# Value product turned round: values as weights, two heads on two column halves, attention output born transposed

## The reference

```
first_block:
    proj = rms_norm(x, attn_norm_gain) @ w_in        # fq fk fv fg dq dk dv
    fox_o = forgetting_attention(fq, fk, fv, fg + bias)   # 16 heads of 64
    dil_o = dilated_attention(rope(dq), rope(dk), dv)     # 16 heads of 64, 3 patterns
    mixed = concat[rms_norm(fox_o, fox_out_gain), rms_norm(dil_o, dil_out_gain)]
    h = x + mixed @ w_out ;  h = h + peer(rms_norm(h, g)) ;  return rms_norm(h)
    # attention of one head:  p = softmax(q k^T / 8 + mask terms);  o = p @ v
second_block (its end):
    gate = sigmoid(rmsnorm(x, ple_norm_g) @ w_ple_gate)
    x = x + gate * (p @ w_ple_proj) ;  return rmsnorm(x, final_norm_g)
```

## Time and profile before

| | |
|---|---|
| median of 3 runs | 2812.62 us (2812.09 to 2813.28) |
| the profiled execution: its time | 2811.79 us |
| its span, first to last instruction | 2810.0 us |
| TensorE busy | 2790.0 us, 99% of the span |
| VectorE, ScalarE, GpSimd busy | 65%, 50%, 25% |
| TensorE's granted clock | 0.999 of full |
| attention's side work | about 174 to 355 us of the span |
| embedding gate | about 2697 to 2810 us |

### The profile page before, as it was taken

One profiled execution on the slowest core, in us unless ns is written; L12 is line 12 of the kernel. 1 busy time (PEld: TensorE's weight loads), 2 busy tenths in 40 slices (PEclk: granted clock), 3 DMA queues, 4 the chain that ended last, 5 costly groups with the idle time before them and its releaser, 6 DMA issues.

```text
span 2810.0 us, 39121 instructions
## 1 busy us (share of the span) xinstructions
PE 2790.0 (99%) x14986; PEld 2403.7 (86%) x14986; DVE 1824.3 (65%) x2904; ACT 1409.5 (50%) x1993; POOL 697.8 (25%) x365
## 2 busy tenths in 40 slices
PE   9999999999999999999999999999999999999998
PEld 7888888888888888888888888888888888999886
DVE  6566766877777755555555555566777876555554
ACT  5445654555555544454444444546655555444454
POOL 0000000488888888800000000001201111000000
PEclk9999999999999999999999999999999999999999
DMA  7653479877777777777677777765665546666664
GB/s 273 211 158 121 142 239 338 240 189 190 191 189 188 190 191 189 190 217 223 209 223 222 212 237 223 238 209 185 185 183 157 160 153 190 188 190 189 184 197 154
DMA packets 199018, 559.02 MB, mean 199 GB/s; under 512 B 53344, under 2 KB 69872, under 8 KB 195888
## 3 DMA queue, kind: packets, MB, share of 16 engines
q1 hardware_dynamic: 161744, 556.04, 63.6%
q0 software_dynamic: 36944, 0.41, 2.7%
q10 hardware_dynamic: 144, 0.07, 0.0%
HBM read 535.32 MB, written 21.12 MB: 198 GB/s over the span
## 4 chain that ended last, share of the span: by engine, by line
PE 93%; DVE 3%; ACT 2%; issue 1%; DMA 1%; POOL 0%; DVEq 0%; SPq 0%; ACTq 0%
PE bank L535 92%; DVE wlo L946 1%; ACT whi L1675 1%; PE bank L547 1%; DMA raw<-in_w_pq 0%; DMA raw<-in_w_dv 0%; DVE tmpc L949 0%; ACT EB L1675 0%; ACT L1675 0%; DVE aX L981 0%; DVE QKb L949 0%; DVE AT L1200 0%; ACT scr L1675 0%; DVE EB L1008 0%; DVE X L949 0%
## 5 line engine op out<-in xcount | busy, mean ns | idle before, releaser
L946 DVE TENSOR_TENSOR wlo<-raw,whi 128x1024 fp32r<-128x1024 f32 (+1 forms) x965 | 1188.9, 1234 | 852.7 <-ACT whi L1675 849.5
L1675 ACT ACTIVATE whi<-raw 128x1024 fp32r<-128x1024 f32 (+1 forms) x967 | 1017.3, 1054 | 992.7 <-PE bank L535 974.9
L535 PE MATMUL bank<-aX,whi 128*128 128x512 f32 (+1 forms) x4000 | 968.9, 392 | 0.8 <-DVE aX L981 0.8
L535 PE MATMUL bank<-whi,aX 128*128 128x512 f32 x3008 | 932.5, 390 | 0.5 <-DVE aX L949 0.4
L535 PEld LDWEIGHTS bank<-aX,whi 128*128 128x128 f32 (+1 forms) x4000 | 728.1, 188 | 142.0 <-issue 3.0
L535 PEld LDWEIGHTS bank<-whi,aX 128*128 128x128 f32 x3008 | 565.0, 188 | 119.3 <-DVE aX L949 1.5
L1635 POOL DMA_INDIRECT gate_scratch<-gate,place x256 | 585.7, 2288 | 256.1 <-DMA gate_scratch<-HB 178.4
L535 PE MATMUL bank<-wlo,aX 128*128 128x512 f32 x1504 | 585.5, 390 | 2.2 <-DVE wlo L946 2.2
L535 PEld LDWEIGHTS bank<-aX,wlo 128*128 128x128 f32 (+1 forms) x3984 | 513.3, 191 | 21.0 <-DVE wlo L946 0.8
L535 PE MATMUL bank<-aX,wlo 128*128 128x256 f32 (+1 forms) x3984 | 529.4, 284 | 0.3 <-DVE wlo L946 0.2
L535 PEld LDWEIGHTS bank<-wlo,aX 128*128 128x128 f32 x1504 | 282.6, 188 | 62.2 <-DVE wlo L946 4.2
(11 more groups left out here) (229 smaller groups left out, 1833.4 us busy)
## 6 DMA issues: line engine op xcount, KB each, us to landing
raw<-in_w_down SPq DMA_DIRECT2D x256, 512.0 KB, 3.7
raw<-in_w_up SPq DMA_DIRECT2D x256, 512.0 KB, 4.3
raw<-in_w_in SPq DMA_DIRECT2D x176, 512.0 KB, 3.8
raw<-in_w_out SPq DMA_DIRECT2D x32, 512.0 KB, 3.8
gate_scratch<-HB SPq DMA_DIRECT2D x16, 1024.0 KB, 7.6
raw<-in_w_pq SPq DMA_DIRECT2D x32, 512.0 KB, 5.4
raw<-in_w_o SPq DMA_DIRECT2D x32, 512.0 KB, 4.3
raw<-in_w_pg SPq DMA_DIRECT2D x32, 512.0 KB, 4.2
```

What stands on the lines that cost most here:

```text
L535: return e.matmul(o, lhsT, rhs, start=start, stop=stop, skip_group_check=True)
L946: e.tensor_tensor(wlo[:, s, 0:n], raw[:, r, 0:n], whi[:, s, 0:n].bitcast(F32), ALU.subtract).then_inc(s_lo, 1)
L1675: return e.activation(o, i, f, **k)
```

## The change

**Value product.** `VV` (128 keys x 64 features of head x) is now the weight and `PB` streams: 256 columns (both query blocks) for key block 0 and 128 for key block 1. Head 0 writes PSUM partitions 0 to 63, head 1 partitions 64 to 127 of the same bank, with the heads innermost in the loop. The output is features x tokens, so no transposes of `TM` follow: `MIX_TURN`, its TensorE transposes, `high_two` and `low_two` for dil and fox are gone, and so is `VR`. ScalarE writes the high part and VectorE the low part straight from the value product's bank (phase D), in `mD` and `mF`, which lie over dead parts of the query/key tiles and of `TM`.

**Normalization.** The reciprocal sum belongs to a token, which is now a column, so it is applied before the transposes: GpSimd multiplies `EB` by the reciprocals in two instructions per pair (2x128 and 2x256 columns), and phase C waits for it (`s_gn`). For f pairs the reciprocal moves to a phase B at +1, C to +3 and D to +4.

**Sums of squares.** ScalarE squares the value product's bank into `sq`, GpSimd adds the squares up in `acc` (14 additions of 128x256), and TensorE sums over the partitions by a product with ones (`mix_sums`, ticks 89 and 106). The eight 128x512 squares are gone.

**Embedding gate.** Group i's multiply, add and square are done inside group i+1's `pg` units, each behind a split (`gated`, `gated_square`); only the last group's stay at the end.

```diff
-MIX_TURN = {86: ("dil", 0), 87: ("dil", 1), 90: ("dil", 2), ...
-MIX_SQUARE = {84: ("dil", 0), 85: ("dil", 1), 102: ("fox", 0), 103: ("fox", 1)}
-MIX_SUM = {92: "dil", 104: "fox"}
+MIX_ROW = {89: "dil", 106: "fox"}
...
-        for phase, n in zip("ABCD", (0, 1, 3, 4)) if kind == "d" else zip("ACD", (0, 2, 3)):
+        for phase, n in zip("ABCD", (0, 1, 3, 4)):
...
             if phase == "C":
-                if kind == "d":
-                    w.wait_ge(s_cn, 4 * sum(k == "d" for k, _, _ in PAIRS[:q + 1]))
-                else:
-                    w.wait_ge(s_ex, 4 * q + 4)
+                w.wait_ge(s_gn, q + 1)
...
-                for t in range(2):
+                for kt in range(2):
                     for x in range(2):
-                        for kt in range(t + 1):
-                            ov = mm(b[:, 128 * t + 64 * x:128 * t + 64 * x + 64],
-                                    PB[:, 2 * (q % 3) + x, (t + kt) * 128:(t + kt) * 128 + 128],
-                                    VV[:, kt, vb + 64 * x:vb + 64 * x + 64], kt == 0, kt == t)
+                        ov = mm(b[64 * x:64 * x + 64, 128 * kt:256], VV[:, kt, vb + 64 * x:vb + 64 * x + 64],
+                                PB[:, 2 * (q % 3) + x, 256 * kt:256 + 128 * kt], kt == 0, kt == 1)
...
+        def mix_sums(name):
+            q = PLACE[name[0], 7]
+            w.wait_ge(s_sa, ADDED[q])
+            b = vacant(mfill[name])
+            for t in range(2):
+                sm = mm(b[:, t * 128:t * 128 + 128], acc[name[0]][:, t * 128:t * 128 + 128], ones[:, 0:128], True, True)
+            sm.then_inc(s_sm, 1)
...
             if phase == "D":                                  # VectorE
-                w.wait_ge(s_turn, 4 if q < 4 else 8)
-                tt(TM[...], banks[b][:, 0:256]..., d2[:, :, 4:6]..., ALU.mult).then_inc(s_free[b], 1)
+                w.wait_ge(s_ph, q + 1)
+                e.scalar_tensor_tensor(o[:, 256:512], banks[b][:, 0:256], cols[:, c:c + 1], o[:, 0:256].bitcast(F32),
+                                       ALU.mult, ALU.subtract).then_inc(s_free[b], 1)
...
+        def normalize(q):                                     # GpSimd
+            w.wait_ge(s_rd, q + 1)
+            for c, k in ((slice(0, 128), 4), (slice(128, 384), 5)):
+                p = E[:, :, c]
+                last = e.tensor_tensor(p, p, d2[:, :, k:k + 1].to_broadcast([128, 2, c.stop - c.start]), ALU.mult)
+            last.then_inc(s_gn, 1)
+        def add_squares(q, kind, pair):
+            if pair:
+                w.wait_ge(s_sqp, DONE.index(q) + 1)
+                w.wait_ge(s_sa, ADDED[q] - 1)
+                e.tensor_tensor(acc[kind], acc[kind], sq[:, ADDED[q] % 2, :], ALU.add).then_inc(s_sa, 1)
...
+            if phase == "D":                                  # ScalarE
+                w.wait_ge(s_ov, q + 1)
+                act(junk, banks[b][:, 0:256], ACT.Square).then_inc(s_sqp, 1)
+                w.wait_ge(s_turn, 8 if kind == "f" else 4)
+                if kind == "d":
+                    w.wait_ge(s_lg, 2 * over(q) + 2)
+                act(o[:, 0:256], banks[b][:, 0:256], ACT.Copy, scale=cols[:, c:c + 1]).then_inc(s_ph, 1)
...
         for i in range(4):                                    # VectorE, embedding gate
-            steps(G["pg", i])
-            ...  multiply and add of group i behind pp, for both token blocks
+            for j, u in enumerate(G["pg", i].units):
+                step(u)
+                if i and j < 2:
+                    gated(i - 1, j)
+            steps(G["pp", i])
+        for t in range(2):
+            gated(3, t)
```

More of the change, by code:

```diff
@@ L218, in _build @@
     rsin = attc[:, 912:928].rearrange("p (t i) -> p t i", t=2)
-    fz, fu, fw, fm = (fgs[:, i, :] for i in range(4))
+    fz, fu, fw, fm = (fgs[0:16, i, :] for i in range(4))
+    acc = {"d": fgs[:, 0, :], "f": fgs[:, 1, :]}
+    sq = fgs[:, 2:4, :]
     A.close()
     B_ = ExitStack()
-    alloc(B_, "below_VV", [128, 2 * 4096])
-    VR = alloc(B_, "VR", [128, 2, D], F32R)
-    alloc(B_, "below_dil", [128, 2 * 2048])
+    alloc(B_, "below_fox", [128, 4096])
+    mF = alloc(B_, "mF", [128, 8, 512], F32R)
+    alloc(B_, "below_dil", [128, 2 * 4096])
     mD = alloc(B_, "mD", [128, 8, 512], F32R)
@@ L319, in _build @@
                 hfill[q, phase] = [plan.side()]
-        if t in MIX_TURN:
-            plan.turn(*MIX_TURN[t], plan.side())
+        if t in MIX_ROW:
+            mfill[MIX_ROW[t]] = plan.side()
+    mfill["fox"] = plan.side()
     for name, part in (("wd", range(4, 8)), ("wf", range(4))):
@@ L404, in tile, with over @@
         if name == "dil":
-            return mD[:, kt, :]
+            return mD[:, kt // 2 + kt % 2 * 4, :]
         if name == "fox":
-            return VR[:, kt // 2, 1024 + kt % 2 * 512:1536 + kt % 2 * 512] if kt < 4 else aX[:, 8 + kt, :]
+            return mF[:, kt, :]
         return aX[:, mix_row(kt) if name == "mix" else kt, :]
[L410 to L413, removed]
+    PLACE = {(kind, pair): q for q, (kind, pair, _) in enumerate(PAIRS)}
+    DONE = [q for t in HEAD_TICKS for q, _, _, phase in HEADS[t] if phase == "D"]
+    ADDED = {q: n + 1 for n, q in enumerate(x for x in DONE if PAIRS[x][1])}
+    def over(q):
+        pair = PAIRS[q][1]
+        return max(PLACE["d", p] for p in (pair // 2 * 2, pair // 2 * 2 + 1))
     def decay_cols(p):
@@ L666, in tick @@
                         heads(q, kind, pair, phase)
-            if u in MIX_TURN:
-                mix_turn(*MIX_TURN[u])
+            if u in MIX_ROW:
+                mix_sums(MIX_ROW[u])
             if u == ROWS0 + 4:
@@ L974, in row_scale, with mix_scale @@
             e.reciprocal(st[:, o:o + 2], st[:, 20:22]).then_inc(s_rinv, 1)
+        def mix_scale(name, o):
+            j = next(sums)
+            b, _ = mfill[name]
+            w.wait_ge(s_sm, 1 if name == "dil" else 2)
+            e.tensor_copy(st[:, 16:18], banks[b][:, 0:256].rearrange("p (t c) -> p t c", t=2)[:, :, 0]).then_inc(s_free[b], 1)
+            evacuated(mfill[name])
+            e.tensor_scalar(st[:, 16:18], st[:, 16:18], 1.0 / 1024, EPS, ALU.mult, ALU.add).then_inc(s_rsum, 2)
+            w.wait_ge(s_root, j + 1)
+            e.reciprocal(st[:, o:o + 2], st[:, 20:22]).then_inc(s_rinv, 1)
         def low_two(name, kp):
@@ L1009, in heads @@
                                                ALU.add, ALU.min, d[:, t:t + 1]).then_inc(s_free[b] if t else s_mx, 1)
-            if phase == "B":
+            if phase == "B" and kind == "d":
                 for x in range(2):
@@ L1018, in heads @@
                 e.reciprocal(d2[:, :, 4:6], d2[:, :, 2:4]).then_inc(s_rd, 1)
-            if phase == "C" and kind == "f":
+            if phase == "B" and kind == "f":
                 w.wait_ge(s_ex, 4 * q + 4)
@@ L1240, in step @@
                     heads(q, kind, pair, phase)
[L1241 to L1246, removed]
+            if u in MIX_ROW:
+                mix_scale(MIX_ROW[u], 24 if MIX_ROW[u] == "dil" else 26)
             if u == G["dq", 0].first + 1:
@@ L1594, in _, with gated @@
                 tt(o, banks[b], o, ALU.add).then_inc(s_free[b], 1)
-        row_scale(4, D, 40, 8)
-        for i in range(4):
-            steps(G["pg", i])
[L1598 to L1611, removed]
+        row_scale(4, D, 36, 4)
+        def gated(i, t):
+            g = G["pp", i]
+            b, _ = g.fills[t]
+            o, x = scr2[:, t, i * 512:i * 512 + 512], X2[:, t, i * 512:i * 512 + 512]
+            if i == 3 and t == 0:
+                w.wait_ge(s_pt, 1)
+            else:
+                ready(g)
+            evacuated(G["pg", i].fills[t])
+            tt(o, banks[b], o, ALU.mult).then_inc(s_free[b], 1)
+            evacuated(g.fills[t])
+            tt(x, x, o, ALU.add).then_inc(s_x4, 1)
+        for i in range(4):
+            for j, u in enumerate(G["pg", i].units):
[5 more added lines that the diff above has]
+            gated(3, t)
+        row_scale(4, D, 44, 4)
         w.wait_ge(s_row2, 16)
@@ L1624, in _ @@
         w = Gate(e)
+        def normalize(q):
+            E, d2 = EB[:, 2 * (q % 3):2 * (q % 3) + 2, :], dn[:, 2 * (q % 3):2 * (q % 3) + 2, :]
+            w.wait_ge(s_rd, q + 1)
[8 more added lines that the diff above has]
+                e.tensor_tensor(acc[kind], acc[kind], sq[:, ADDED[q] % 2, :], ALU.add).then_inc(s_sa, 1)
+        for t in HEAD_TICKS:
+            for q, kind, pair, phase in HEADS[t]:
+                if phase == "B":
+                    normalize(q)
+                if phase == "D":
+                    add_squares(q, kind, pair)
         w.wait_ge(s_ht, 32)
@@ L1755, in heads @@
                     act(PB[:, i, :], banks[b][:, 0:384], ACT.Copy).then_inc(s_free[b], 1)
+            if phase == "D":
+                name = "fox" if kind == "f" else "dil"
+                b, n = hfill[q, "D"][0]
+                o, c = tile(name, pair), GAIN[name] + pair
+                w.wait_ge(s_ov, q + 1)
+                if pair:
```

(19 more changed lines are left out.)

34 lines of the change are left out of this document (12 added, 22 removed).

## The result

The changed kernel takes 2817.56 us (median; 2815.61 to 2821.09, 14 runs), the kernel before beside it 2812.23 us (2811.56 to 2813.28, 14 runs). The ratio is 1.0019 with a 95% interval of 1.0011 to 1.0027: slower by 0.2%, where 0.3% faster was forecast. The profiled execution took 2816.7 us, span 2814.8, 4.8 more than before.

What follows compares the result with a forecast made beforehand. TensorE, busy for 99% of the span, was taken as the bound. 6.3 + 3.6 - 1.0 + 0.6 - 2.0 + 1.5 = 9.0 us saved gave a median of 2803.6 us; own range 2801 to 2807, whole range 2797 to 2810.

Steps and rivals of the forecast that it cites:

- the pairing of the column halves: Value product: the two heads' column halves run together, so D streams for 0.66 us instead of costing 1.29.
- the gate: Embedding gate: three of four waits at column group starts go, with uncovered weight loads, winning 1.5 us.
- 6.3 + 3.6 - 1.0: TensorE's side work: value product saves 6.3 us, dropped mix turns save 3.6, the new sums of squares cost 1.0.
- cheap entry: Rival on the value product: column halves entered without drain, saving 10.1 us, and GpSimd in time; 2797.8 us, chance 0.19.
- no pairing: Rival on the value product: column halves don't run together, loss of 4.3 us instead of gain; 2814.2 us, chance 0.14.
- uncovered loads: Rival on the value product: column halves hide no weight loads, 4.8 us more; 2808.4 us, chance 0.05.
- GpSimd's normalization, 2.0 us: Attention: TensorE waits 1.1 us at pair 0 and 0.6 at pair 4, plus 0.3 for slowed splits.
- The price of the link, 3.3 us: From reciprocal to transposes: GpSimd's multiplications 2.0 us, plus 1.2 for giving way to a VectorE split, plus 0.1.
- these are the tightest dilated pairs, and fox's C is a tick later than before: Normalization: pairs 0 and 4, with 2.2 and 2.7 us available, were taken as the places where TensorE waits.
- GpSimd late: Rival: normalization takes 4.5 us, behind two splits; TensorE waits 1.8 us in all 16 pairs; 2830.4 us, chance 0.05.
- The 13 us of free time in 40 cover it: cost nothing.: Attention: VectorE's wait of some 1 us for ScalarE in every D stays hidden; up to 16 us without the cover.
- I count 0.6 us back: Bank waits: with C one tick later, A's 0.4 us wait for D's bank and smaller ones go, winning 0.6 us.

Runs made afterwards that it cites:

- the kernel without the link: Changed kernel, GpSimd's same multiplications and additions run on a dead tile, transposes not waiting for them, output not normalized: 2805.73 us.
- the unit of room: Changed kernel with phases C and D of the last four fox pairs one unit later: 2806.73 us.
- the 0.8 us that it costs with room: Changed kernel with last four pairs' C and D one unit later and ScalarE's copies first, without GpSimd's normalization: 2799.36 us, against 2800.17 with it.
- Turning ScalarE's order around: Exponentials of fox pairs 5, 7, 9, 11 one unit later, behind the previous pair's copies; with last four pairs' C and D one unit later: 2800.17 us.
- the one with the gate alone: Kernel before with only the embedding gate's part of the change: 2810.88 us, ratio 0.9995.
- the kernel with ScalarE's order alone: Changed kernel, phases kept, ScalarE's exponentials of fox pairs 5, 7, 9, 11 one unit later, behind the previous pair's copies: 2812.64 us.
- the one with all of D later: Changed kernel with last four pairs' C and D one unit later, and the first twelve pairs' D one unit later too: 2809.75 us.

## Why the prediction was wrong

**Right** were the pairing of the column halves, D with A behind it (0.49 us shorter, forecast 0.43), and the gate. Over all of attention TensorE's side work is about 9.4 us shorter, waits left out, by the distances of its starts; the forecast was 6.3 + 3.6 - 1.0 = 8.9. The rivals on the product fell: cheap entry (0.32 us from the last normal start to the first product), no pairing, uncovered loads.

The forecast was 2803.6 and the time 2817.6, 14.0 us more. The kernel without the normalization parts this: it takes 2804.4, where the sum without its 2.0 gives 2801.6. So 11.2 us of the miss are the normalization and 2.8 all other terms.

**The step that failed first is GpSimd's normalization, 2.0 us; it costs 13.2.** The price of the link, 3.3 us, was near: 2.7 to 3.8 from the reciprocal's start to C. Its place was wrong: "these are the tightest dilated pairs, and fox's C is a tick later than before". I took fox's extra unit for room and followed it to no row. In fox pairs C had waited for the exponentials alone; now the reciprocal stands between too, and it is late by what VectorE does ahead of it, 3.0 us at pair 12. And the last four pairs have no other pair's work between their phases: from A to C pair 12 has 9.3 us (291.2 to 302.9 less the wait), the fox pairs among the dilated ones 12.1 to 13.8. There TensorE waits as in the rival "GpSimd late", but in four pairs instead of sixteen, 8.0 us, and not by the rival's cause: not a link of 4.5 us, but a shorter way with more of VectorE's work ahead of the link. What GpSimd's load does to VectorE was put at 0.3 us, for splits; the D waits that came with the normalization are 3.7. Shown by the kernel without the link (11.8), the unit of room (10.8), and the 0.8 us that it costs with room.

**Second: "The 13 us of free time in 40 cover it: cost nothing."** They are not where the work is queued. D's second piece on ScalarE and VectorE's wait for it push masks, exponentials and copies back one behind the other, and the copies had half a microsecond to spare. But by itself this costs little: without the normalization TensorE waits 0.9 us for copies, where it waited 0.4 in the kernel before, and 1.5 us for parts of weights, where it waited for none in attention. That is 2.0 us of the 2.8. The rest of the 4.6 us of D waits needs the normalization on top. Turning ScalarE's order around took all of them away and won 4.9 us in the changed kernel and 6.6 with room.

**Third, small: bank waits, "I count 0.6 us back".** The 0.4 of the earlier trace rows did go. But the second set of transposes of `TM`, which stands in both kernels, waits 1.2 us for D's low part (1.5 without the normalization), where it had waited 0.6 for the multiplication. It is 0.2 lost instead of 0.6 won.

**The balance** of the two spans, between the same products. Ahead of attention: -0.3. Attention: +5.1. From there to the gate: +1.7; TensorE waits 1.8 us there behind attention, 1.0 of it for a transfer of keys, where it waited 0.2. The gate: -1.7. Together that is the 4.8. Inside attention side work is -9.4 and idle time 15.0 - 1.4 = +13.6, which makes 4.2; the 0.9 to the 5.1 is no more than what idle time leaves out of eleven more waits, up to 0.16 us of each. Waits for the keys were between 0 and 1.1 us in the other kernels too (0.6 in the one with the gate alone), so they aren't shown to be the change's.

## What to carry to other kernels

Where a link is put into a chain, write down for each class of places that it comes to when its input is ready, what stands ahead of it on its engine and when its consumer is due; the class with the shortest way between its phases decides, not the one that was tightest before. A share of free time says nothing about an engine that works in order: look for the smallest distance between a result and its user among all that is queued behind the added work. A shorter stream on the bounding engine brings every consumer forward, so the schedule around it has to be laid out again: here one unit more for four pairs and one exchange on ScalarE turned a loss of 5 us into a gain of 12.

## What the runs showed of the hardware

The granted clock can fall behind short waits. In the kernel with ScalarE's order alone, TensorE was busy for 2.81 of 5 us with a wait of 2.2 us for GpSimd in them, and then the clock fell (windows view, and the timeline behind it):

```profile
295.00:300.00 5.00, 2.81 (x23) 2.49 (x21) 4.05 (x6) 1.02 (x4) 3.49 (x2) 1.00 0.81 215
300.00:305.00 5.00, 5.00 (x24) 4.03 (x24) 1.72 (x4) 2.74 (x4) 0.00 (x0) 0.66 0.28 100
...
301.61 2.90 PE L541 MATMUL bank<-aX,whi 128*128 128x512 f32 x8
```

Eight products of 512 columns took 2.9 us, partly at the lower level of 1.2 GHz; at 2.4 GHz they follow by 0.23. Another 10 us had 0.86. That fits its attention, which is only 2.0 us shorter than the changed kernel's with 4.6 us less of waits. The kernel with the normalization on VectorE had a clock of 0.79 in the 16 us with its longest wait (3.6 us), the one with all of D later 0.83 in 10. In the profile of the changed kernel the clock stayed at 1.00 behind waits of up to 2.8 us, so a wait doesn't always bring it. Whether such dips make that kernel's wide spread was not shown.

GpSimd and VectorE slow each other, also where they work on different data: multiplications of 256 columns took 1515 ns on average on the exponentials and 1444 on the dead tile, where those of the earlier trace rows took 744 at the median; and the longest mask of VectorE rose from 0.42 to 1.26 us.
